# A decoder layer on one core: the front in two halves with loads from two queues, three turned tiles copied by two engines, and a block's rows moved behind the first scores

## The reference

```
c-dependent rows: mod = silu(c) @ w_ada + b_ada     -> 9 parts: shift, scale, gate for three sub-layers
h = x + 1/2 gate_f1 * SwiGLU_1(RMSNorm(x) * (1 + scale_f1) + shift_f1)
u = RMSNorm(h) * (1 + scale_m) + shift_m
[q_a | kv_a | k_pe | glu_in | gates] = u @ w_in
A = attention(q, k, v) @ w_attn_out      latent keys: k = kv_lat @ w_uk, per-head norm of q and k, rope
B = silu(LayerNorm(DWConv31(GLU(glu_in)))) @ w_conv_out
h = h + gate_m * ((sigmoid(gA) A + sigmoid(gB) B) @ w_out)
y = h + 1/2 gate_f2 * SwiGLU_2(...)
```

## Time and profile before

| | |
|---|---|
| median of 3 runs | 1172.36 us (1171.31 to 1172.78) |
| the profiled execution, its time | 1171.14 us |
| its span in the trace | 1169.3 us |
| TensorE busy | 1136.3 us, 97% |
| VectorE, ScalarE busy | 776.7 us, 66%; 584.2 us, 50% |

### The profile page before, as it was taken

How to read it: one execution, slowest core, us unless ns; L and a number is a source line. 1 busy time by engine, 2 the same in 40 slices (tenths; PEclk the granted TensorE clock), 3 DMA queues, 4 the chain that set the end, 5 groups by cost and what they waited for, 6 DMA issues and landing times.

```text
span 1169.3 us, 26044 instructions
## 1 busy us (share of the span) xinstructions
PE 1136.3 (97%) x9613; PEld 1099.2 (94%) x9613; DVE 776.7 (66%) x1316; ACT 584.2 (50%) x1148; POOL 61.9 (5%) x128
## 2 busy tenths in 40 slices
PE   6699999999999999999999999999999999999998
PEld 3699999999898999999999999999999999999997
DVE  1655554467774788888888888888667666555542
ACT  1454443336674855555545454555566445444432
POOL 1000000010000000101010110101010000000000
PEclk8899999999999999999999999999999999999999
DMA  9588678947443251021211202031247773565551
GB/s 328 191 297 288 194 248 269 348 173 229 124 148 112 76 154 43 7 77 27 57 41 40 58 24 76 11 108 42 73 127 252 232 255 114 176 187 175 179 186 64
DMA packets 165295, 169.84 MB, mean 145 GB/s; under 512 B 25710, under 2 KB 143473, under 8 KB 165191
## 3 DMA queue, kind: packets, MB, share of 16 engines
q1 hardware_dynamic: 164695, 167.88, 45.7%
q10 hardware_dynamic: 512, 0.82, 0.2%
HBM read 167.13 MB, written 2.49 MB: 145 GB/s over the span
## 4 chain that ended last, share of the span: by engine, by line
PE 91%; DVE 2%; SPq 2%; ACT 2%; issue 1%; DMA 1%; DVEq 0%; POOL 0%; ACTq 0%
PE PS L1774 27%; PE PS L1776 26%; PE PS L1775 26%; SPq L439 2%; PE PS L1833 2%; PE PS L2148 1%; PE PS L2149 1%; PE PS L2173 1%; DMA raw<-in_w_ffn_in 1%; PE PS L1915 0%; ACT wH L681 0%; PE PS L2096 0%; PE PS L2034 0%; PE PS L2144 0%; DVE u L1153 0%
## 5 line engine op out<-in xcount | busy, mean ns | idle before, releaser
L1112 DVE TENSOR_TENSOR wL<-raw,wH 128x1024 fp32r<-128x1024 f32 (+2 forms) x208 | 245.8, 1188 | 213.4 <-ACT wH L681 211.9
L681 ACT ACTIVATE wH<-raw 128x1024 fp32r<-128x1024 f32 (+2 forms) x208 | 213.3, 1029 | 254.2 <-PE PS L1776 229.3
L1774 PE MATMUL PS<-uH,wH 128*128 128x264 f32 x1024 | 295.5, 289 | 10.0 <-DVE uL L1163 6.5
L1775 PE MATMUL PS<-uL,wH 128*128 128x264 f32 x1024 | 292.9, 286 | 0.0
L1776 PE MATMUL PS<-uH,wL 128*128 128x264 f32 x1024 | 292.4, 286 | 0.0
L1774 PE MATMUL PS<-wqH,kTH 128*128 128x336 f32 (+2 forms) x768 | 255.5, 333 | 0.0
L1776 PE MATMUL PS<-wqH,kTL 128*128 128x336 f32 (+2 forms) x768 | 246.3, 321 | 0.0
L1775 PE MATMUL PS<-wqL,kTH 128*128 128x336 f32 (+2 forms) x768 | 245.9, 320 | 0.0
L1774 PEld LDWEIGHTS PS<-uH,wH 128*128 128x128 f32 x1024 | 195.3, 191 | 12.0 <-issue 7.9
L1775 PEld LDWEIGHTS PS<-uL,wH 128*128 128x128 f32 x1024 | 195.6, 191 | 0.1
L1776 PEld LDWEIGHTS PS<-uH,wL 128*128 128x128 f32 x1024 | 194.8, 190 | 0.0
(11 more groups left out here) (322 smaller groups left out, 1513.5 us busy)
## 6 DMA issues: line engine op xcount, KB each, us to landing
raw<-in_w_ffn_in SPq DMA_DIRECT2D x88, 512.0 KB, 3.6
adaw<-in_w_ada SPq DMA_DIRECT2D x72, 512.0 KB, 6.5
raw<-in_w_ffn_out SPq DMA_DIRECT2D x32, 512.0 KB, 3.8
raw<-in_w_in SPq DMA_DIRECT2D x32, 512.0 KB, 4.7
kv<-in_cache_kv_latent SPq DMA_DIRECT2D x128, 128.0 KB, 2.0
raw<-in_w_ffn_out SPq DMA_DIRECT2D x16, 384.0 KB, 3.3
raw<-in_w_attn_out SPq DMA_DIRECT2D x8, 512.0 KB, 5.6
raw<-in_w_conv_out SPq DMA_DIRECT2D x8, 512.0 KB, 4.4
```

The source lines that it names most:

```text
L681: f(wH[:, k, 0:width], raw[:, k, 0:width], ACT.Copy).then_inc(w_hi, 1)
L1112: v.tensor_tensor(wL[:, k, 0:width], raw[:, k, 0:width], wH[:, k, 0:width].bitcast(F32), ALU.subtract).then_inc(w_lo, 1)
L1774: mm(dst, a[0], b[0], start=start, stop=False)
L1775: mm(dst, a[0], b[1], start=False, stop=False)
```

## The change

It has five parts. (1) In the front the blocks of `w_ada` come as scale 0, shift 0, scale 1, shift 1, in places of their own (`ADA_SLOT` 3, 4, 5, 6), and chunks are laid out anew: 0 and 1 hold row blocks 0 to 3 of up and gate columns, 2 and 3 row blocks 4 to 7. ScalarE issues chunks 0 and 1, ahead of `w_dw` and the constants; SyncE issues 2 and 3 behind all four blocks. `scales`, `prenorm` and `shifted` work on halves of the row blocks, and TensorE multiplies the first half while the second is made (`halves`), with blocks 2 and 3 of `w_ada` between. The gains and taps are turned there as well; GpSimd adds all eight squares. (2) The copies of the turned key weight, of the first keys and of both query tiles are cut in two: ScalarE takes the first half of the banks, VectorE the second (a new semaphore `turned`). (3) `qabs` uses banks 7 and 6; the second tile of queries follows the first, and the new scores come behind `zst`, in bank 1. (4) The rows of block `ADA_FFN` go behind the scores of head 2, its turn on VectorE behind the mask of head 2. (5) In the convolution's out-projection VectorE's last gated sum stands ahead of the two `lo`.

```diff
-ADA_ORDER = [2, 3, 0, 1, 4, 5, 8, 9, 6, 7, 10, 11, 12, 13, 14, 15, 16, 17]
-ADA_SLOT = [0, 1, 2, 3, 4, 5, 3, 4, 5, 3, 4, 5, 3, 6, 0, 3, 5, 6]
+ADA_ORDER = [2, 0, 3, 1, 4, 5, 8, 9, 6, 7, 10, 11, 12, 13, 14, 15, 16, 17]
+ADA_SLOT = [3, 4, 5, 6, 3, 4, 5, 3, 4, 5, 3, 4, 5, 6, 0, 3, 5, 6]
...
-SUMMED = (4, 5, 3)
+SUMMED = (7, 5, 3)
...
+                    for half in range(2):
+                        ada_load(2 * half)
+                        ada_load(2 * half + 1)
+                        if half == 1:
+                            for m in range(2):
+                                chunk(q0, 2 + m, v[:, 4:KT, ds(m * FF, 256)], 4, 256, first=True)
...
+            for m in range(2):
+                act.dma_start(raw[:, m, 0:SLOT].rearrange("p (k n) -> p k n", k=4),
+                              wview(x["w_ffn1_in"])[:, 0:4, ds(m * FF, 256)]).then_inc(w_in[m], 16)
+            act.dma_start(dwrow[:, :], x["w_dw"]).then_inc(in_row, 16)
+            act.dma_start(const[:, P:C_N], x["const"][:, P:C_N]).then_inc(in_row, 16)
...
+            root(0, 3)
+            hi(0, 0, SLOT)
             act.wait_ge(vec_ps, 1)
-            f(vecT[:, :], PS[:, 7, 72:72 + V_N], ACT.Copy)
-            f(wdw[:, :, :].rearrange("p a b -> p (a b)"), PS[:, 7, 200:200 + KT * CW], ACT.Copy).then_inc(vec_sb, 1)
-            root(0, 0)
-            act.wait_ge(ada_used, 2)
-            hi(0, 0, SLOT)
-            shifted(0)
-            for k in range(1, 4):
-                hi(0, k, SLOT)
+            f(vecT[:, :], PS[:, 7, P:P + V_N], ACT.Copy).then_inc(vec_sb, 1)
+            hi(0, 1, SLOT)
+            shifted(0, 0)
+            hi(0, 2, SLOT)
+            shifted(0, 1)
+            hi(0, 3, SLOT)
...
+            filled(act, "wuk")
+            f(wukT[:, :, :].rearrange("p a b -> p (a b)")[:, 0:1024], PS[:, 4:6, :].rearrange("p a b -> p (a b)"),
+              ACT.Copy).then_inc(use_act, 1)
             ahead(Q_UQV + 1, 2)
-            ahead(Q_UQV + 1, 3)
-            filled(act, "wuk")
-            f(wukT[:, :, :].rearrange("p a b -> p (a b)"), PS[:, 4:8, :].rearrange("p a b -> p (a b)"),
+            filled(act, "kt0")
+            f(kT[:, 0:8, 0:128], PS[0:QK, 0:2, :].rearrange("p a (h n) -> p (a h) n", n=128),
               ACT.Copy).then_inc(use_act, 1)
             query_sq(0)
-            by_head("kt0", kT, 0, 0)
+            ahead(Q_UQV + 1, 3)
...
+            invert(0)
+            dve.wait_ge(vec_sb, 1)
+            for half in range(2):
+                if half == 0:
+                    lo(0, 0, SLOT)
+                mod_columns(2 * half)
+                scales(0, half)
+                if half == 1:
+                    lo(0, 2, SLOT)
+                mod_columns(2 * half + 1)
+                prenorm(0, half)
+                lo(0, 2 * half + 1, SLOT)
...
+            filled(dve, "wuk")
+            v.tensor_copy(wukT[:, :, :].rearrange("p a b -> p (a b)")[:, 1024:2048],
+                          PS[:, 6:8, :].rearrange("p a b -> p (a b)")).then_inc(turned, 1)
...
+            filled(dve, "kt0")
+            v.tensor_copy(kT[:, 8:H, 0:128], PS[0:QK, 2:4, :].rearrange("p a (h n) -> p (a h) n", n=128)
+                          ).then_inc(turned, 1)
...
+            for t, b in ((0, 2), (1, 6)):
+                filled(dve, f"qt{t}")
+                v.tensor_scalar(qT[:, 8:H, 128 * t:128 * t + 128],
+                                PS[0:QK, b:b + 2, :].rearrange("p a (h n) -> p (a h) n", n=128),
+                                gqk[0:QK, :], None, ALU.mult).then_inc(turned, 1)
...
+                    if j == m == 1:
+                        mixed(j, m)
...
+            def halves(q, half, m, b, base=None, between=None):
+
+                k = 2 * half + m
+                pe.wait_ge(w_lo, 4 * q + k + 1)
+                for n in range(2):
+                    for kt in range(4 * half, 4 * half + 4):
+                        if base is not None and n == 0:
+                            pe.wait_ge(u_ready, base + kt + 2)
+                        c = slice((kt - 4 * half) * 256 + 128 * n, (kt - 4 * half) * 256 + 128 * n + 128)
+                        i_ = product(PS[:, b + n, 0:T], (wH[:, k, c], wL[:, k, c]), (uH[:, kt, :], uL[:, kt, :]),
+                                     kt == 0, kt == KT - 1)
+                    if n == 0 and between is not None:
+                        mod_rows(between)
+                i_.then_inc(w_used, 1)
...
+                if norm == 0:
+                    pe.wait_ge(g_free, g0 + 1)
+                    for half in range(2):
+                        for m in range(2):
+                            halves(q0, half, m, 2 * m, half, 3 if m > half else None)
+                            if half == m == 0:
+                                mod_rows(2)
+                                pe.wait_ge(vec_sb, 1)
+                        if half == 0:
+                            pe.wait_ge(in_row, 32)
+                            pe.wait_ge(mod_turned, 3)
+                            for kt in range(KT):
+                                i_ = tr(PS[:, 6, 256 + CW * kt:256 + CW * kt + CW], dwrow[:, P * kt:P * kt + P],
+                                        ident[0:CW, 0:CW])
+                            i_.then_inc(vec_ps, 1)
...
-            read(pe, "qabs")
             pe.wait_ge(g_free, G_GLU + 6)
             pe.wait_ge(tok_done, 4)
             by_head(0, qtok[:, 0, :, :])
-            for kt in range(2):
-                mm(PS[0:NB, 4, 0:128], kvTn[:, kt, :], qabs[:, :, kt, :], start=(kt == 0), stop=False)
-            mm(PS[0:NB, 4, 0:128], krTn[:, :], qrT[0:ROPE, :, :].rearrange("p h b -> p b h"), start=False, stop=True
-               ).then_inc(use_ps, 1)
-            pe.wait_ge(rest_sb, 5)
+            read(pe, "qabs")
             pe.wait_ge(tok_done, 5)
             by_head(4, qtok[:, 1, :, :])
             read(pe, "qt0")
+            pe.wait_ge(turned, 3)
             pe.wait_ge(prod_done, FT + 10)
             for kt in range(KT):
                 i_ = tr(PS[0:CW - 1 + NB, 2 + kt // 4, 128 * (kt % 4):128 * (kt % 4) + 128],
                         zbuf[:, kt, SEQ:CW - 1 + T], ident)
             i_.then_inc(use_ps, 1)
-            mod_rows(ADA_FFN)
+            for kt in range(2):
+                mm(PS[0:NB, 1, 0:128], kvTn[:, kt, :], qabs[:, :, kt, :], start=(kt == 0), stop=False)
+            mm(PS[0:NB, 1, 0:128], krTn[:, :], qrT[0:ROPE, :, :].rearrange("p h b -> p b h"), start=False, stop=True
+               ).then_inc(use_ps, 1)
             read(pe, "qt1")
 
 
             def scores(hd):
                 b = hd % 2
+                if hd == 0:
...
                 if hd == 0:
+                    mod_rows(ADA_FFN)
                     pe.wait_ge(zst_done, 2)
```

More of the change, by code:

```diff
@@ L917, in _ @@
             filled(act, "qabs")
-            for m, bank in ((0, 7), (1, 0)):
+            for m, bank in ((0, 7), (1, 6)):
                 i_ = f(qabs[:, :, :, m:H:2],
@@ L1119, in _, with scales @@
             dve.sem_inc(prod_done, 2)
[L1120 to L1123 removed]
+            for bank in (6, 2, 7):
+                v.memset(PS[:, bank, 0:P], 0.0).then_inc(ada_zero, 1)
+            def scales(n, half=None):
                 part, g = ((CF1, V_G1), (CM, V_GM), (CF2, V_G2))[n]
+                a, e = (0, KT) if half is None else (4 * half, 4 * half + 4)
                 own.wait()
                 own.done(v.scalar_tensor_tensor(
[L1127 to L1128 removed]
+                    out=amod[:, n, a:e, :], in0=mod[:, KT * part + a:KT * part + e, :], scalar=1.0,
+                    in1=vecT[:, g + a:g + e].unsqueeze(2).to_broadcast([P, e - a, NS]), op0=ALU.add, op1=ALU.mult))
             def half_gate(part):
@@ L1740, in _ @@
                                     ).then_inc(g_free, 1)
-                own.end(2)
             with dve.Fori(0, 2) as j:
@@ L2041, in _ @@
             read(pe, "kt0")
+            pe.wait_ge(turned, 2)
             glu(2, 0)
```

171 lines of the change are left out of this document (79 added, 92 removed).

## The result

The changed kernel takes **1160.46 us** (median of 4 runs, 1159.05 to 1162.97) where before takes 1171.84 (median of 4 runs: the three of the table above and one of 1168.67). The medians lie 11.4 us apart; the ratio on record is 0.9913, with a 95% interval from 0.9896 to 0.9930: faster by 10 us, 8 to 12. The forecast was 1162.1, range 1157.5 to 1167. The profiled execution took 1162.97, the slowest of the four; its span is 1161.1.

What follows compares the result with a forecast made beforehand. TensorE, busy 97% of the span, was taken as the bound; its waits and low clock gave 6.4 + 0.9 + 2.0 + 1.0 = 10.3 us, so 1172.36 - 10.3 = 1162.1 us, range 1157.5 to 1167.

Steps and rivals of the forecast that it cites:

- The late DMA engine, chunk 2 at 41.1: Front loads: one of sixteen DMA engines, about 3 us behind, ends unchanged; chunk 2 lands at 40.6 plus 0.5 for alternating queues.
- the flat 24 GB/s: Front, before: DMA rate from 39.0 to about 41.7, read as one of sixteen DMA engines still working alone.
- Front, 6.4 (3.5 to 8): Front: the first column group of FFN 1 ends at 54.4 in place of 60.8, 6.4 us gained, bounds 3.5 and 8.
- this wait decides: Front: TensorE is free at 45.4, the second half ready at 46.5, so waiting for it decides, by one microsecond.
- rival 1: Front: the first half, at the lower clock, holds up the second; front gains 3.2 us, total 1165.3; chance beyond range 0.15.
- group 0: Front: the first group of columns of FFN 1, 96 products, 11.6 us at full clock, put as ending at 60.8 before.
- Keys, 0.9 (0 to 1.6): Turned key weight and first keys: halved copies gain 1.6 us, VectorE's delay leaves 0.9; bounds 0 and 1.6.
- Rival 4: Keys and queries: the halves bring nothing because VectorE's delay takes it all; total 1165.0, inside the first forecast's range (chance 0.68).
- Queries, scores and block, 2.0 (1 to 2.8): Queries to first turned probabilities: idle gaps go, 1.8 us, plus 0.2 for VectorE; 2.0 us, bounds 1 and 2.8.
- So I give nothing for the clock: Queries: tile 0's turn, at clock 0.55 behind narrow products that stay, was credited no gain from the clock.
- Convolution out, 1.0: Convolution's out-projection: VectorE's last gated sum done at 934, so TensorE's 1.04 us wait goes; 1.0 us gained.
- Rival 3: Front: not faster, as ScalarE is held by its own issues and csil comes after 29.6; chance 0.04.

Runs made afterwards that it cites:

- split load: The changed kernel with w_dw loaded by two DMAs, of 16 and 15 rows, in place of one of 31: 1155.72 us, ratio 0.9867 to before.
- the block at its old place: The changed kernel with the rows of ADA_FFN back behind the turned queries and their turn ahead of the first mask: 1160.10 us, ratio 0.9922 to before.
- the whole copies: The changed kernel with ScalarE copying turned key weight, first keys and both query tiles whole, VectorE's halves left out: 1164.13 us, ratio 0.9946 to before.
- the front alone: The kernel before with only part 1 of the change: 1165.36 us against 1171.16, ratio 0.9954.
- one queue: The changed kernel with chunks 0 and 1 issued by SyncE in place of ScalarE: 1161.29 us, ratio 0.9917 to before.
- the two parts: The kernel before with only part 1 (1165.36 us, 5.4 us faster), and with only parts 2 to 5 (1164.56 us, 6.4 us faster).

## Why the forecast was right, point by point

- **The late DMA engine, chunk 2 at 41.1:** landed at 41.19 in after. The split load shows what it cost: without 31 rows in one DMA the landing is 36.79. The forecast took the engine as given and was right to leave its end where it was. (It reads the flat 24 GB/s as reaching to about 41.7; the 28 slices of the earlier trace rows end at 41.4. Nothing in the sum hangs on it.)
- **Front, 6.4 (3.5 to 8):** the fifth block starts at 176.98, 175.38 and 176.71 in three profiles of the old front, mean 176.4, and at 171.49, 170.66, 170.55, 170.24, 170.76 and 169.94 in six of the new one (the block at its old place and the whole copies among them), mean 170.6. That is 5.8, and by the runs of the front alone 5.4 (3.4 to 7.4). That the first half's products run while the second is made was right, and the size 0.6 to 1 too large. The step that failed is "this wait decides". The forecast has TensorE free at 45.4 and so the second half's `uL`, ready at 46.5, as what it waits for; its own sign was a first product at 46 to 47 behind `uL`. The `uL` was ready at 46.60, but the first product came at 32.55 in place of 32, the products from there to 38.3 ran at half the clock, and TensorE was free only at 47.41. This is rival 1, with its first microsecond, and not only in that execution: in five of these six profiles TensorE comes to the second half without idle time, and only with the whole copies, where the first product was at 31.16, did it wait, 0.46 us. That the sum still came within a microsecond is due in part to the two ends lying so close. Also, the profile of before that the sum starts from was the slowest of the three in its front, by 0.3 to 1.6; and its group 0 ended at 60.63, not 60.8.
- **Keys, 0.9 (0 to 1.6):** 0.97 (31.45 to 30.48; one profile of the old order has 31.54). It is made of 1.9 up to the turned rows of the samples' queries (forecast 1.6) and 0.95 given back in the last GLU group (forecast 0.7), in small gaps at the starts of chunks, of which the largest is at 351.44, with a wait of 0.26 for `wL`. Rival 4, that the halves bring nothing, was wrong: without them 1.5 us go.
- **Queries, scores and block, 2.0 (1 to 2.8):** from 17.15, 17.07, 17.01 to 13.62, of which 1.3 to 1.5 is the turns of tile 0 at the lower clock (3.25 to 3.40 in place of 1.95); 2.1 are left, as forecast, 0.83 by the block. "So I give nothing for the clock" was the mis-sized step: in six of nine profiles of the new order that 1.5 comes too.
- **Convolution out, 1.0:** 1.28 (24.79 to 23.51), in every profile of the table.
- **Rival 3, ScalarE held by its own issues:** it was: 3.67 us for the constants, and `csil` at 12.44 where the forecast says no later than 12. Its price was nothing, since the second block comes at 28.48 anyway; with `csil` at 7.89 (one queue) the time is the same.
- The sum of the stages, 5.8 + 0.97 + 2.1 + 1.28 = 10.1, comes with the 1.5 for the clock at the queries, which most executions have, to 11.6, near the 11.4 of the medians and the 11.8 of the two parts; with the 1.3 that the pages may give back it is 10.3, near the 10.2 of the ratio. The forecast had neither of these two clock terms, and that they nearly cancel is luck. A clock that differs from one execution to the next, in the front (up to 1.6), at the queries (1.3 to 4), over the pages (3) and in FFN 2 (1.4), is what keeps the account from closing better than to 1 us.

## What to carry to other kernels

Look in the front of a kernel for a load whose slowest dimension is an awkward number of rows (here 31): 124 KB in such a load cost 5 us in the new front and 3 to 4 in the old one, a third to half of what the whole change brought, and the tell-tale is a flat, low rate in the DMA's slices while a large load is still to land. When a front is cut into halves, the second half's chain (landing, rounding, remainder, normalisation, 5.2 to 5.4 us here) comes close behind TensorE's own work, and a still earlier first product brought nothing here. A gain that a single profile shows in a stretch with narrow products should be compared over two or three profiles before it is believed, since the clock there moves it by more than most edits.
